# Constants, the first normalization and the cached keys' decays in one front stage with four tile buffers; the decays reach attention by way of DRAM

## The reference, cut to what matters

```python
def _rmsnorm(x, g):
    y = xf * lax.rsqrt(jnp.mean(xf * xf, axis=-1, keepdims=True) + EPS)
    return (y * g.astype(jnp.float32)).astype(x.dtype)
...
    xn = _rmsnorm(x, norm_g)
    proj = xn @ w_in
...
        past_logf = cache_logf[page_table].reshape(Bs, -1, C_HEADS)
...
    csum = jnp.cumsum(jnp.concatenate([past_logf, logf], axis=1), axis=1)
    ck = jnp.transpose(csum, (0, 2, 1))
    cq = ck[:, :, P:]
    s = s + cq[..., :, None] - ck[:, :, None, :]
```

## Time and profile before

| | before |
|---|---|
| median of 3 runs | 3149.75 us (3144.71 to 3150.09) |
| the profiled execution | 3147.39 us, of them span 3145.6 us |
| busy in the span | PE 2821.2 us (90%), DVE 1612.8, POOL 1379.8, ACT 1022.5 |
| mean granted clock of PE | 0.947 |

### The profile page before, as it was taken

How to read it: one execution, slowest core, us unless ns; L and a number is a source line. 1 busy time by engine, 2 the same in 40 slices (tenths; PEclk the granted TensorE clock), 3 DMA queues, 4 the chain that set the end, 5 groups by cost and what they waited for, 6 DMA issues and landing times. The chain is left out here.

```text
span 3145.6 us, 46329 instructions
## 1 busy us (share of the span) xinstructions
PE 2821.2 (90%) x17133; PEld 2247.7 (71%) x17133; DVE 1612.8 (51%) x2154; ACT 1022.5 (33%) x1721; POOL 1379.8 (44%) x986
## 2 busy tenths in 40 slices
PE   3898989859988998988999956999999999998999
PEld 3898989857666997878999944555555555554887
DVE  4223343333454778986555546455455555553432
ACT  5313233222344221221112203454454545444100
POOL 0000000000001576767898835777776777777000
PEclk7899989889999999999999977999999999999999
DMA  4110110106544777888787738887887978873532
GB/s 124 36 34 28 35 34 28 41 26 212 171 149 139 239 265 248 283 256 286 256 268 249 254 107 206 245 214 214 237 225 212 255 211 228 242 203 126 184 121 70
DMA packets 327915, 547.68 MB, mean 174 GB/s; under 512 B 76094, under 2 KB 220130, under 8 KB 319213
## 3 DMA queue, kind: packets, MB, share of 16 engines
q1 hardware_dynamic: 263564, 471.12, 51.2%
q10 hardware_dynamic: 61120, 58.83, 5.4%
q0 software_dynamic: 3008, 14.81, 1.2%
HBM read 449.58 MB, written 95.12 MB: 173 GB/s over the span
## 5 line engine op out<-in xcount | busy, mean ns | idle before, releaser
L1179 POOL TENSOR_TENSOR p_kp<-p_kp,p_qb 128x1024 f32<-128x1024 f32 x256 | 626.7, 2475 | 389.4 <-DMA p_kp<-in_cache_k_dram 306.3
L2025 POOL TENSOR_TENSOR at_acc<-at_acc,at_w 128x512 f32<-128x512 f32 (+3 forms) x576 | 645.2, 1120 | 228.1 <-ACT at_w L2153 163.9
L2188 DVE TENSOR_REDUCE at_mx<-at_mx 128x1 f32<-128x512 f32 (+3 forms) x640 | 382.5, 608 | 426.1 <-PE at_mx L2060 310.6
L112 PE MATMUL p_pb<-p_w,x_xh 128*128 128x256 f32 x2048 | 593.2, 290 | 8.6 <-DVE p_w L1493 8.6
L113 PE MATMUL p_pb<-p_w,x_xh 128*128 128x256 f32 x2048 | 580.7, 284 | 0.0
L114 PE MATMUL p_pb<-p_w,x_xl 128*128 128x256 f32 x2048 | 580.1, 283 | 0.0
L2153 ACT ACTIVATE at_w<-at_st,c_nckt 128x512 f32<-128x512 f32 (+3 forms) x640 | 389.6, 622 | 365.9 <-PE at_st L2086 193.5
L1595 DVE TENSOR_REDUCE p_sc<-p_kp 128x16 f32<-128x1024 f32 x256 | 307.5, 1214 | 224.8 <-POOL p_kp L1179 224.7
L112 PEld LDWEIGHTS p_pb<-p_w,x_xh 128*128 128x128 f32 x2048 | 391.9, 191 | 20.9 <-issue 11.2
L113 PEld LDWEIGHTS p_pb<-p_w,x_xh 128*128 128x128 f32 x2048 | 393.5, 192 | 0.0
L114 PEld LDWEIGHTS p_pb<-p_w,x_xl 128*128 128x128 f32 x2048 | 392.9, 192 | 0.0
(11 more groups left out here) (296 smaller groups left out, 3844.0 us busy)
## 6 DMA issues: line engine op xcount, KB each, us to landing
p_kp<-in_cache_k_dram SPq DMA_DIRECT2D x256, 512.0 KB, 4.9
at_vp<-in_cache_v_dram SPq DMA_DIRECT2D x256, 512.0 KB, 5.6
o_mt<-mixed SPq DMA_DIRECT2D x32, 512.0 KB, 4.8
p_raw<-in_w_in_dram SPq DMA_DIRECT2D x32, 512.0 KB, 6.9
at_q<-qh SPq DMA_DIRECT2D x32, 512.0 KB, 11.3
at_k<-kh SPq DMA_DIRECT2D x32, 512.0 KB, 8.4
l_raw<-in_w_in_dram SPq DMA_DIRECT2D x20, 512.0 KB
mixed<-l_w POOLq DMA_DIRECT2D x8, 1028.0 KB, 4.2
```

The source lines that it names most:

```text
L112: nc.tensor.matmul(out, lhs[0], rhs[0], start=(k == 0), stop=False)
L1179: nc.gpsimd.tensor_tensor(kp[:, g % 4], kp[:, g % 4], qb[:], ALU.mult).then_inc(kmul, 1)
L2025: nc.gpsimd.tensor_tensor(t[:, 512 - wd:512], t[:, 512 - wd:512], W[n % RW][:, 0:wd], ALU.add).then_inc(accd, 1)
L2188: nc.vector.reduce_max(mx[:, u % 2, j, seg:seg + 1], MX[r % 2][:, 0:wd], AX.X).then_inc(mread, 1)
```

## The change

A new stage `front` (tiles f_) takes the place of `setup` and of n0, and does `past`'s work as well; `past` is gone. The tiles get four load buffers (`NX = 4`). SP issues the page table, tile 0, the norm's gain, tiles 1 to 3, then the 26 small loads, then the rest of the tiles. DVE does four scans behind each of the tiles 4 to 11, in place and with the heads innermost, so that a scan now reads and writes every 16th element; before, it wrote a contiguous row. The subtraction moves to POOL as four instructions of 128x1024. PE turns two groups of decays behind each of the tiles 14, 15 and 16 and two at the end; ACT copies them to `dk`, which holds four samples at a time; SP stores it to DRAM in two DMAs of 1 MB. The second half of the copies waits for the first store. The end of the stage waits for the second.

`attention` loads each sample's decays (256 KB) beside its scores, and the new value is taken off the new key's score in `project1`, by two small instructions on DVE. The function `tiles_stage` goes away, as n0 was its only use.

```diff
-def setup(nc, z, a, C):
+def front(nc, z, a, C, D, xh, xl):
...
+    TILES = [(n, P, n * P) for n in range(z.NT)] + [(z.NT, z.B, z.T)]
+    N = len(TILES)
+    NX = 4
+    NG = z.B // z.SB
+    GP, H, PG = z.GP, z.H, z.PG
+    SC0, SC1 = 4, 4 + 4 * NG
...
+        xt = S.sb("x", [P, NX, z.D])
...
+        L = S.sb("l", [GP, NG, P, H])
...
+        dk = S.sb("dk", [P, z.SB, H, PG])
+        tp = S.ps("tp", [P, 2, z.KB, P])
+        pt = [S.ps(f"pt{x}", [P, 512]) for x in range(2)]
...
+        CONSTS_AT, LAMBDA_AT, TOTALS_AT, TURN_AT = 5, 8, 4 + 4 * NG, 14
...
+            def load(n, rows, col):
+                if n >= NX:
+                    sp.wait_ge(xnd, n - NX + 1)
+                src = a["x_prompt"][0, ds(col, rows), :] if rows == P else a["x_sample"][:, 0, :]
+                sp.dma_start(xt[0:rows, n % NX, :], src).then_inc(x_in[n % NX], 16)
+            for n in range(NG):
+                sp.dma_start(idx[:, n:n + 1], a["page_table"][n * z.SB:(n + 1) * z.SB, :].rearrange("b g -> (b g)")
+                             .rearrange("(q o) -> q o", o=1)).then_inc(idx_in, 16)
+            load(*TILES[0])
+            sp.dma_start(gb[:], a["norm0_g"].partition_broadcast(P)).then_inc(g_in, 16)
+            for n in range(1, NX):
+                load(*TILES[n])
+            for dst_, src in loads:
+                sp.dma_start(dst_, src).then_inc(loaded, 16)
+            for n in range(NX, N):
+                load(*TILES[n])
+            for n in range(NG):
+                sp.wait_ge(dcopied, H // 4 * (n + 1))
+                sp.dma_start(D.decay[n * z.SB:(n + 1) * z.SB].rearrange("b p n -> p b n"),
+                             dk[:].rearrange("p b h g -> p b (h g)")).then_inc(dst, 16)
             sp.wait_ge(loaded, 16 * len(loads))
+            sp.wait_ge(dst, 16 * NG)
...
+            nc.gpsimd.memset(ones[:], 1.0).then_inc(made, 1)
+            nc.gpsimd.memset(later[:], 1.0).then_inc(made, 1)
+            pool.wait_ge(idx_in, 16 * NG)
+            for n in range(NG):
+                pool.indirect_dma_start(out=L[:, n].rearrange("q t h -> q (t h)"), out_offset=None,
+                                        in_=a["cache_logf"].rearrange("n p h -> n (p h)"),
+                                        in_offset=bass.IndirectOffsetOnAxis(ap=idx[:, n:n + 1].bitcast(U32), axis=0)).then_inc(l_in, 16)
+            pool.wait_ge(made, 2)
+            nc.gpsimd.affine_select(out=later[:], in_=later[:], compare_op=ALU.is_gt, fill=0.0, base=0,
+                                    pattern=[[-1, GP]], channel_multiplier=1).then_inc(made, 1)
+            pool.wait_ge(made, 3)
...
             pool.wait_ge(copied, 1)
             nc.gpsimd.affine_select(out=C.wst[:], in_=C.wst[:], compare_op=ALU.is_ge, fill=0.0, base=0,
                                     pattern=[[0, z.G], [1, P]], channel_multiplier=-1).then_inc(wmask, 1)
             pool.wait_ge(wmask, 1)
+            pool.wait_ge(l_in, 16 * NG)
+            for n in range(NG):
+                pool.wait_ge(tadd, n + 1)
+                for x in range(2):
+                    hs = slice(H // 2 * x, H // 2 * (x + 1))
+                    nc.gpsimd.tensor_tensor(L[:, n, :, hs], tot[:, n, hs].rearrange("q (o h) -> q o h", o=1).broadcast_to([GP, P, H // 2]),
+                                            L[:, n, :, hs], ALU.subtract).then_inc(dsub, 1)
...
+            def decays(m):
+                n, x = divmod(m, H // 4)
+                act.wait_ge(dturned, m + 1)
+                if n:
+                    act.wait_ge(dst, 16 * n)
+                nc.scalar.activation(dk[:, :, 4 * x:4 * x + 4, :].rearrange("p b h g -> p h b g"),
+                                     pt[m % 2][:, 0:4 * GP].rearrange("p (h b g) -> p h b g", h=4, g=PG), ACT.Copy).then_inc(dcopied, 1)
+            turns = 0
+            for n, rows, col in TILES:
+                act.wait_ge(x_in[n % NX], 16 * (n // NX + 1))
+                if n >= NX:
+                    act.wait_ge(xnd, n - NX + 1)
+                nc.scalar.activation(sq[0:rows], xt[0:rows, n % NX, :], ACT.Square,
+                                     accum_out=st[0:rows, n % NX, 0:1]).then_inc(sqd, 1)
+                act.wait_ge(sqd, n + 1)
+                if n == 0:
+                    act.wait_ge(filled, 3)
+                nc.scalar.activation(st[0:rows, n % NX, 1:2], st[0:rows, n % NX, 0:1], ACT.Sqrt, scale=1.0 / z.D,
+                                     bias=C.eps[0:rows]).then_inc(stdd, 1)
+                if n:
+                    hi(*TILES[n - 1])
+                if n == LAMBDA_AT:
+                    act.wait_ge(loaded, 16 * len(loads))
+                    nc.scalar.activation(t1[:], lam[:], ACT.Abs).then_inc(lnd, 1)
+                    act.wait_ge(lnd, 1)
+                    nc.scalar.activation(t1[:], t1[:], ACT.Exp, scale=-1.0).then_inc(lnd, 1)
+                    act.wait_ge(lnd, 2)
+                    nc.scalar.activation(t1[:], t1[:], ACT.Ln, bias=1.0).then_inc(lnd, 1)
+                if n >= TURN_AT:
+                    for x in range(2):
+                        decays(turns)
+                        turns += 1
+            hi(*TILES[N - 1])
+            for m in range(turns, NG * H // 4):
+                decays(m)
...
+            def scans(m):
+                n, x = divmod(m, 4)
+                if m == 0:
+                    dve.wait_ge(made, 1)
+                    dve.wait_ge(l_in, 16 * NG)
+                for h in range(H // 4 * x, H // 4 * (x + 1)):
+                    last = nc.vector.tensor_tensor_scan(L[:, n, :, h], ones[:], L[:, n, :, h], 0.0, ALU.mult, ALU.add)
+                last.then_inc(scand, 1)
+            def totals():
+                for n in range(NG):
+                    dve.wait_ge(latm, NG)
+                    dve.wait_ge(scand, 4 * (n + 1))
+                    nc.vector.tensor_tensor(tot[:, n, :], L[:, n, P - 1, :], pl[0:GP, n * H:(n + 1) * H], ALU.add).then_inc(tadd, 1)
+            for n, rows, col in TILES:
+                dve.wait_ge(stdd, n + 1)
+                nc.vector.reciprocal(st[0:rows, n % NX, 2:3], st[0:rows, n % NX, 1:2]).then_inc(rcd, 1)
+                dve.wait_ge(rcd, n + 1)
...
+                if n >= 2:
+                    dve.wait_ge(trd, n - 1)
+                nc.vector.scalar_tensor_tensor(out=xn[0:rows, n % 2, :], in0=xt[0:rows, n % NX, :], scalar=st[0:rows, n % NX, 2:3],
+                                               in1=gb[0:rows], op0=ALU.mult, op1=ALU.mult).then_inc(xnd, 1)
+                if n:
+                    lo(*TILES[n - 1])
+                if SC0 <= n < SC1:
+                    scans(n - SC0)
+                if n == CONSTS_AT:
+                    constants()
+                if n == LAMBDA_AT + 1:
+                    rates()
+                if n == TOTALS_AT:
+                    totals()
+            lo(*TILES[N - 1])
+            dve.wait_ge(cdv, 6 + z.G)
...
+            def later_totals():
+                pe.wait_ge(made, 4)
+                pe.wait_ge(scand, 4 * NG)
+                pe.wait_ge(cdv, 2)
+                for n in range(NG):
+                    nc.tensor.matmul(pl[0:GP, n * H:(n + 1) * H], later[:], L[:, n, P - 1, :], start=True, stop=True).then_inc(latm, 1)
+            def decays(m):
+                n, x = divmod(m, H // 4)
+                pe.wait_ge(dsub, 2 * n + x // (H // 8) + 1)
+                if m >= 2:
+                    pe.wait_ge(dcopied, m - 1)
+                elif m == 0:
+                    pe.wait_ge(copied, 1)
+                else:
+                    pe.wait_ge(cdv, 1)
+                for h in range(4):
+                    last = nc.tensor.transpose(pt[m % 2][:, h * GP:(h + 1) * GP], L[:, n, :, 4 * x + h], C.ident[0:GP, 0:GP])
+                last.then_inc(dturned, 1)
+            turns = 0
             pe.wait_ge(picked, 1)
-            for g in range(z.G):
...
-def tiles_stage(nc, z, C, name, x_of, norm_g=None, xh=None, xl=None, mix=None, w_out=None, x_out=None, lsum=None):
...
+        nsl = wf[0:B, 0, :]
...
+                nc.vector.tensor_scalar(nsl, sm[0:B, 0:z.H], -1.0, None, ALU.mult).then_inc(fcopy, 1)
...
-def past(nc, z, a, C, out):
...
+            dve.wait_ge(schain, sampled_steps(NCK))
+            dve.wait_ge(fcopy, 4)
+            nc.vector.tensor_tensor(snew[:], snew[:], nsl, ALU.add).then_inc(schain, 1)
...
-        sc = S.sb("sc", [P, H * PG])
+        sc, dk = S.sb("sc", [P, H * PG]), S.sb("dk", [P, H * PG])
...
                 sp.dma_start(sc[:], D.sc[b]).then_inc(sc_in, 16)
+                sp.dma_start(dk[:], D.decay[b]).then_inc(sc_in, 16)
...
-                    dve.wait_ge(sc_in, 16 * (b + 1))
+                    dve.wait_ge(sc_in, 32 * (b + 1))
-                    nc.vector.tensor_tensor(sd[:, :, 0:PG], sc[:].rearrange("p (h g) -> p h g", g=PG), C.decay[:, b, :, 0:PG], ALU.add).then_inc(sdd, 1)
```

(54 more changed lines are left out.)

387 lines of the change are left out of this document (61 added, 326 removed).

## The result

| | before | after |
|---|---|---|
| median | 3149.92 us (3141.54 to 3156.73, 12 runs) | 3132.33 us (3123.55 to 3139.69, 12 runs) |
| the profiled execution | 3147.39, span 3145.6 | 3128.79, span 3127.1 |
| granted clock of PE | 0.947 | 0.947 |

The account below looks back on a forecast made before the run. Start and `past` were taken as chains of engines waiting for each other, not PE-bound. Removing `past` saves 38.3, the front ends 11.2 later: 27.1 less than 3147.39 is 3120.3, plus 2.4 for the median, 3123 us; range 3112 to 3137.

Parts of the forecast that it names:

- The gain from `past`, -38.3: Stage between `project1` and attention: lies wholly on the path between two barriers, so removing it saves all 38.3 us.
- Tile 4, forecast scaled at 27.4: Front: tile 4 lands at 24.3 behind the small loads; square, root, inversion and scale end at 27.4 us.
- The sum of DMA shares, 24.3: Front's start: DMA work queued before tile 4, plus tile 4, makes 21.3 us from about 3 on, landing at 24.3.
- Tiles 5 to 12, forecast 36.4: Front: DVE bounds at 4.0 us a tile, 32.0 for eight; constants 1.9, rates 0.5 and ACT's table loads 2 added.
- rival 4: Front's scans: strided writes make the kernel slower than before if a scan takes 1.17 us or more; chance 0.03.
- The tail, forecast 33.3: Front after tile 12's scale: chain of turning, copies and two stores puts layer 0's first load 33.3 us later.
- 2 for contention: Front's tail: scales of tiles 13 and 14 wait beside POOL's subtractions; 2 us taken, bounds nothing and 4.9 each.
- The two small additions in `project1` and a copy for an add in SD: `project1` and attention's step SD: edits costed at nothing, below 0.5 us together.
- 27.1: Whole kernel: forecast net gain in us, from 38.3 saved by removing `past` and a front 11.2 longer.
- 2 (front hides all): Front: ends where the old stage ended, so the whole 38 us shows, 3112 us; chance 0.19.
- 3 (front much slower): Front: saturated DMA engines and the pitch's cost move its end by 10 to 14 more, 3135 us; chance 0.21.
- 5: Attention's start: gets longer by what `past` lost, so no gain shows, about 3148 us; chance 0.04.

Follow-up runs that it names:

- f2: Against the changed kernel, GpSimd's two gathers wait until tile 1 is scaled instead of for the indices; 3131.91 us (one run).
- f1: Against the changed kernel, small loads go out four at a time behind the loads of tiles 4 to 10, constants made at tile 12; 3121.68 us median.
- g1: Against the changed kernel, the four subtractions of the totals stand on DVE behind the totals instead of on POOL; 3131.55 us (one run).
- s1: Against the changed kernel, SD's one-input copy of the new score is an addition of a column of zeros; 3129.86 us median.
- s3: Against the changed kernel, GpSimd's fill of Q2's rows is split into four fills, SD's copy left as it is; 3128.51 us (one run).
- m1: Against the kernel before, only SD's small addition becomes the one-input copy of the new score; 3160.13 us (one run).
- c1: Against the changed kernel: s1, f1, half stores, squares ahead of decays, and DVE subtractions one a tile at tiles 12 to 15; 3108.96 us median.

## Why the prediction was right in sign and 9 us too low

**The gain from `past`, -38.3.** As forecast: no stage is left there, and attention's first product is 19.75 us behind its first load, before (1885.28) and after (1860.46).

**Tile 4, forecast scaled at 27.4, measured 34.3.** This is the step that failed most. "Then come the 26 small ones at 0.56, to 18.3, and only then tile 4" took SP's issue time from a stage in which nothing else filled the DMA engines; beside the gather and behind the tile loads the 26 took 23.3 (4.15 to 27.50) in place of 14.65, one of them 7.39. The sum of DMA shares, 24.3 for the landing, assumed that tile 4 is in the queue while the engines catch up. It was not: its issue came at 27.50, and it landed within 3.8 of that, as tiles do. f2 gives 3.7 of these 6.9 us back by the gather alone, and f1 takes 11.2 off the front by the order. The prediction named "after 30" as what would speak against it; the square started at 31.32.

**Tiles 5 to 12, forecast 36.4, measured 35.4** (34.3 to 69.75). The pace is 3.79, not 4.0, and ACT's table loads cost DVE 2.7 where I had added 2.

**The strided scans (rival 4, 0.03)** took 0.32 each, as in the sum: refuted.

**The tail, forecast 33.3 and 2 for contention, measured 34.4.** Order and mechanism as written: square 15 behind two copies, the second store last. Contention was 2.9, shown by g1. The 3.39 of tile 13's scale is above the "3 us" that I had named as a sign against it: the mechanism was right and the wait longer. The front's end, 104.15, is just outside the 95 to 104 that I had named for it.
The Trainium skill (SBUF — State Buffer, "Who interferes with whom") says that a DVE instruction with two SBUF inputs contends with a GpSimd instruction that reads SBUF. The trace agrees, with 3.39 against 1.28.

So the front is 16.3 longer, not 11.2: +6.9, -1.0 and -0.9 make the 5.0. The two small errors happened to take 1.9 us off the large one.

**"The two small additions in `project1` and a copy for an add in SD are below 0.5 us together."** The second failed step: 4.5 us, shown by s1, s3 and m1. I looked at the instruction's duration without a neighbour. Its row had a maximum of 706 ns beside a median of 180, and I did not ask what a one-input form would wait for.
The Trainium skill (SBUF — State Buffer, "Who interferes with whom") also says that a copy can enter a mode in which it and GpSimd exclude each other, while an instruction with two SBUF inputs contends only with a GpSimd instruction that reads SBUF. The runs agree on both: beside the fill, which only writes, the copy takes 1.49 and the addition takes 0.18. I had the rule at hand and applied it to the tail alone.

**The ledger.** Front 5.0, the copy's wait 4.5, the stretch at the lower clock 1.5, the untouched middle -2.8, the output layer 0.3: 8.5, where 27.1 - 18.5 = 8.6 is to be explained. The middle's -2.8 is within what it varies by between profiles, so no effect of the change can be read from it; that it brought the total nearer to the forecast is luck.

**The other rivals.** 2 (front hides all) is refuted for this kernel, but c1 does it: its front is 6.6 shorter than the old one. 3 (front much slower) had part of the truth, its saturated DMA engines: their share was 1.00 from 2.5 to 17.5 us. But it cost by holding up SP's issue, and not by a late landing: from 17.5 to 27.5 the share was 0.32, with tile 4's load not yet issued. 5 is refuted by the 19.75.
